# Down projection of a fused decoder step: two tiles interleaved with a lag, operands re-ordered

## What is computed

```python
def conv_ffn(h, buf, w_gate, w_up, conv_w, conv_b, w_down):
    T = h.shape[1]
    u = h @ w_gate
    upad = jnp.concatenate([buf.astype(u.dtype), u], axis=1)
    c = conv_b + sum(conv_w[j] * upad[:, j:j + T] for j in range(CONV_W))
    y = (jax.nn.gelu(c) * (h @ w_up)) @ w_down
    return y, upad[:, -(CONV_W - 1):]
```

## Time and profile before

| | |
|---|---|
| device time, median of 3 runs | 1554.88 us (1554.34 to 1556.92) |
| profiled execution, its own time | 1551.94 us |
| its span in the profile | 1550.2 us |
| instructions | 31361 |
| TensorE matmul busy | 1452.9 us (94%) |
| VectorE, ScalarE, GpSimd busy | 936.7, 675.3, 564.4 us |
| granted TensorE clock, mean | 0.977 |

### The profile page before, as it was taken

One profiled execution on the slowest core, in us unless ns is written; L12 is line 12 of the kernel. 1 busy time (PEld: TensorE's weight loads), 2 busy tenths in 40 slices (PEclk: granted clock), 3 DMA queues, 4 the chain that ended last, 5 costly groups with the idle time before them and its releaser, 6 DMA issues.

```text
span 1550.2 us, 31361 instructions
## 1 busy us (share of the span) xinstructions
PE 1452.9 (94%) x11260; PEld 1326.7 (86%) x11260; DVE 936.7 (60%) x1496; ACT 675.3 (44%) x1263; POOL 564.4 (36%) x561
## 2 busy tenths in 40 slices
PE   7999998889999999998899999998979999998997
PEld 6899898879999999997896656665969899998997
DVE  4742446579888884226647744442569988886223
ACT  5323335355666663223522444442254666664211
POOL 3332112325454443431341044441415454453343
PEclk9999999989999999999999999999989999998999
DMA  4232222213322322223221089980212322321221
GB/s 157 70 130 87 103 89 91 78 44 106 109 90 99 108 75 71 79 94 118 74 88 45 1 252 286 284 253 28 82 47 96 110 90 99 108 82 58 93 81 75
DMA packets 55608, 160.14 MB, mean 103 GB/s; under 512 B 7554, under 2 KB 25475, under 8 KB 54227
## 3 DMA queue, kind: packets, MB, share of 16 engines
q1 hardware_dynamic: 49362, 137.82, 26.8%
q0 software_dynamic: 6144, 20.98, 4.3%
HBM read 150.72 MB, written 8.05 MB: 102 GB/s over the span
## 4 chain that ended last, share of the span: by engine, by line
PE 75%; DVE 12%; issue 7%; ACT 3%; POOL 2%; ACTq 0%; POOLq 0%; DVEq 0%
PE lin L2055 33%; PE lin L2341 23%; PE lin L2519 4%; PE px L2596 2%; PE px L2560 2%; DVE a_l L1707 1%; PE px L2507 1%; PE px L2564 1%; POOL w_l L669 1%; DVE x L1516 1%; DVE tb L1510 1%; PE px L2254 1%; PE px L2527 1%; PE px L2120 1%; PE lin L2473 1%
## 5 line engine op out<-in xcount | busy, mean ns | idle before, releaser
L669 POOL TENSOR_TENSOR w_l<-w_raw,w_h 128x1024 fp32r<-128x1024 f32 (+1 forms) x62 | 172.8, 2789 | 376.4 <-ACT w_h L786 255.1
L2055 PE MATMUL lin<-xg_h,w_h 128*128 128x272 f32 x960 | 226.3, 311 | 43.0 <-DVE xg_l L1334 24.2
L2055 PE MATMUL lin<-xg_l,w_h 128*128 128x272 f32 x960 | 210.2, 294 | 0.0
L2055 PE MATMUL lin<-xg_h,w_l 128*128 128x272 f32 x960 | 210.0, 294 | 0.0
L2055 PEld LDWEIGHTS lin<-xg_h,w_h 128*128 128x128 f32 x960 | 159.5, 195 | 55.9 <-DVE xg_l L1334 17.8
L664 POOL TENSOR_TENSOR w_l<-w_raw,w_h 128x1024 fp32r<-128x1024 f32 (+2 forms) x39 | 99.4, 2549 | 222.3 <-ACT w_h L786 222.3
L2341 PE MATMUL lin<-xq_h,wq_r 128*128 128x272 f32 x864 | 176.6, 292 | 1.9 <-ACT part L1032 1.8
L786 ACT ACTIVATE w_h<-w_raw 128x1024 fp32r<-128x1024 f32 (+2 forms) x77 | 83.3, 1086 | 209.0 <-PE lin L2055 190.6
L2341 PE MATMUL lin<-xq_h,w_h 128*128 128x272 f32 x576 | 166.6, 289 | 4.1 <-DVE xq_l L1650 4.1
L2341 PE MATMUL lin<-xq_h,w_l 128*128 128x272 f32 x576 | 166.7, 289 | 0.0
L2341 PE MATMUL lin<-xq_l,w_h 128*128 128x272 f32 x576 | 166.2, 288 | 0.0
(11 more groups left out here) (360 smaller groups left out, 3125.9 us busy)
## 6 DMA issues: line engine op xcount, KB each, us to landing
wq_raw<-w SPq DMA_DIRECT2D x36, 1024.0 KB, 4.9
w_raw<-w SPq DMA_DIRECT2D x67, 512.0 KB, 3.3
w_raw<-w SPq DMA_DIRECT2D x30, 704.0 KB, 4.0
pages<-cache SPq DMA_DIRECT2D x128, 160.0 KB, 3.7
pages<-cache POOLq DMA_DIRECT2D x128, 160.0 KB, 3.7
St<-state SPq DMA_DIRECT2D x4, 1024.0 KB, 5.2
gla_s<-St SPq DMA_DIRECT2D x4, 1024.0 KB, 3.9
w_raw<-w SPq DMA_DIRECT2D x4, 576.0 KB, 4.2
```

Source lines behind the costliest of these rows:

```text
L669: g.tensor_tensor(w_l[:, p % 2, 0:n], w_raw[:, p % 2, 0:n], w_h[:, p % 2, 0:n].bitcast(F32), ALU.subtract).then_inc(w_lo, 1)
L2055: last = mm(lin[:, 2 * out_set + half, 0:HALF], w[:, slot, (w0 + k) * P:(w0 + k + 1) * P], v[:, ch, half * HALF:(half + 1) * HALF], start= ...
```

## The change

1. The high parts of operands 0, 1 and 2 get places of their own (`a_hs`: unused bytes behind `xg_l`, the place of `rstd_x`, and bytes behind `gl`; `cs` and `cb` move up by 256 bytes). They no longer wait for product 3 of the last pair.
2. ScalarE and VectorE take the 22 operands in another order in and behind the last pair, and ScalarE's `split_hi(pb+2)` comes behind all of them.
3. TensorE takes the first two down tiles together: tile 0's chunks 0 to 10, with tile 1's chunks 0 to 10 seven chunks behind (`LAG_D`), then the second halves of tile 0 and of tile 1. The order of the loads of the first four down panels follows. The hardware loop covers tiles 2 to 5; tile 6 is written out.
4. At the start of the FFN, ScalarE's `split_hi(pa+2)` comes ahead of `rstd`.
5. VectorE makes `input_lo(6)`, the last activation operand of the pairs, ahead of `sums` of pair 1 instead of behind it.

```diff
+        rstd_x_off = pos[0]
         rstd_x = keep("rstd_x", [P, 2, HALF])
...
-        cs = at("cs", E + 8736, [P, FC, NSEQ, 2])
-
+        cs = at("cs", E + 8992, [P, FC, NSEQ, 2])
+        a_hs = [at("a_h0", A0 + 32640, [P, NT], F32R), at("a_h1", rstd_x_off, [P, NT], F32R), at("a_h2", E + 6816, [P, NT], F32R)]
+        a_hs += [a_h[:, k, :] for k in range(3, FC)]
...
+        LAG_D = 7
...
-                sp_.dma_start(w_raw[:, (pb + 1) % 2, :], io["w11"][16 * layer + 1]).then_inc(raw_ready[(pb + 1) % 2], 16)
-                load_run(io["w11"], pb + 2, 16 * layer + 2, 14)
+                sp_.dma_start(w_raw[:, (pb + 1) % 2, :], io["w11"][16 * layer + 2]).then_inc(raw_ready[(pb + 1) % 2], 16)
+                load_panel(pb + 2, io["w11"][16 * layer + 1])
+                load_panel(pb + 3, io["w11"][16 * layer + 3])
+                load_run(io["w11"], pb + 4, 16 * layer + 4, 12)
...
-                    act.wait_ge(w_used, used(pb - 1) + (4 if k < 16 else 5))
+                    if k > 2:
+                        act.wait_ge(w_used, used(pb - 1) + (4 if k < 16 else 5))
...
+                split_hi(pa + 2)
                 rstd(n_stat, D, rstd_x, rstd_p)
-                split_hi(pa + 2)
...
                 part(None, j, 0)
+                operand_hi(0)
+                operand_hi(1)
                 part(None, j, 1)
                 split_hi(pb)
                 part(None, j, 2)
                 gelu(None, j - 1)
-                for k in range(2):
-                    operand_hi(k)
+                operand_hi(2)
+                operand_hi(3)
                 part(None, j, 3)
-                for k in range(2, 6):
-                    operand_hi(k)
+                operand_hi(4)
+                operand_hi(5)
                 first_tap(None, j)
                 operand_hi(6)
                 split_hi(pb + 1)
-                for k in range(7, 10):
-                    operand_hi(k)
                 gelu(None, j)
-                for k in range(10, 14):
+                for k in range(7, FC):
                     operand_hi(k)
                 split_hi(pb + 2)
-                for k in range(14, FC):
-                    operand_hi(k)
...
                 sum_lo(None, 0, 6)
+                input_lo(6)
                 sums(None, 1)
-                input_lo(6)
                 values(None, 0)
...
                 sum_lo(None, j, 6)
+                operand_lo(0)
+                operand_lo(1)
                 product(None, j - 1)
                 values(None, j)
-                for k in range(2):
-                    operand_lo(k)
+                operand_lo(2)
+                operand_lo(3)
                 up_first(None, j)
-                for k in range(2, 7):
-                    operand_lo(k)
+                operand_lo(4)
                 conv(None, j)
-                for k in range(7, 10):
-                    operand_lo(k)
+                operand_lo(5)
+                operand_lo(6)
                 product(None, j)
-                for k in range(10, FC):
+                for k in range(7, FC):
                     operand_lo(k)
...
+                for ch in range(FC // 2 + LAG_D):
+                    if ch < FC // 2:
                         pe.wait_ge(op_l, ops0 + PRODUCTS + ch + 1)
-                        last = tile_matmuls((pb + k) % 2, tb_ % 2, a_h, a_l, (ch,), w0=ch - k * FC // 2, start=ch == 0, stop=ch == FC - 1)
+                        last = tile_matmuls(pb % 2, tb_ % 2, a_hs, a_l, (ch,), w0=ch, start=ch == 0, stop=False)
+                        if ch == FC // 2 - 1:
+                            last.then_inc(w_used, 1)
+                    if ch == LAG_D:
+                        take_panel(pb + 1)
+                        free_set(tb_ + 1)
+                    if ch >= LAG_D:
+                        last = tile_matmuls((pb + 1) % 2, (tb_ + 1) % 2, a_hs, a_l, (ch - LAG_D,), w0=ch - LAG_D, start=ch == LAG_D, stop=False)
+                last.then_inc(w_used, 1)
+                for m in range(2):
+                    take_panel(pb + 2 + m)
+                    for ch in down(1):
+                        pe.wait_ge(op_l, ops0 + PRODUCTS + ch + 1)
+                        last = tile_matmuls((pb + m) % 2, (tb_ + m) % 2, a_hs, a_l, (ch,), w0=ch - FC // 2, start=False, stop=ch == FC - 1)
                     last.then_inc(w_used, 1)
...
+                with pe.Fori(0, 2) as i:
+                    for m in (2, 3):
+                        whole_tile(i, m)
+                whole_tile(None, 6)
```

More of the change, by code:

```diff
@@ L1706, in operand_lo @@
                     dve.wait_ge(op_h, ops0 + PRODUCTS + k + 1)
[L1707 removed]
+                    v.tensor_tensor(a_l[:, k, :], a[:, k, :], a_hs[k][:].bitcast(F32), ALU.subtract).then_inc(op_l, 1)
                 step.wait()
@@ L2055, in tile_matmuls @@
                             last = mm(lin[:, 2 * out_set + half, 0:HALF], w[:, slot, (w0 + k) * P:(w0 + k + 1) * P],
-                                      v[:, ch, half * HALF:(half + 1) * HALF],
+                                      (v[ch] if isinstance(v, list) else v[:, ch, :])[:, half * HALF:(half + 1) * HALF],
                                       start=start and k == 0 and m == 0, stop=stop and k == n - 1 and m == 2)
@@ L2374, in ffn @@
                 down = lambda k: range(k * FC // 2, (k + 1) * FC // 2)
-                for k in range(2):
-                    take_panel(pb + k)
-                    if k == 0:
-                        free_set(tb_)
-                        pe.wait_ge(u_out, outs0 + 2 * PAIRS - 1)
-                    for ch in down(k):
-                        pe.wait_ge(op_l, ops0 + PRODUCTS + ch + 1)
-                        last = tile_matmuls((pb + k) % 2, tb_ % 2, a_h, a_l, (ch,), w0=ch - k * FC // 2, start=ch == 0, stop=ch == FC - 1)
-                    last.then_inc(w_used, 1)
@@ L2384, in ffn @@
-                with pe.Fori(0, DC // 2 - 1) as i:
-                    for m in (1, 2):
-                        for k in range(2):
-                            pe.wait_ge(w_lo, i * 4 + lo_parts(pb + 2 * m + k + 1))
-                            if k == 0:
-                                pe.wait_ge(evac, i * 2 + (tb_ + m - 1))
-                            tile_matmuls((pb + k) % 2, (tb_ + m) % 2, a_h, a_l, down(k), start=k == 0, stop=k == 1).then_inc(w_used, 1)
+                take_panel(pb)
@@ new lines, in ffn, with whole_tile @@
+                last.then_inc(w_used, 1)
[4 more added lines that the diff above has]
+                        last = tile_matmuls((pb + m) % 2, (tb_ + m) % 2, a_hs, a_l, (ch,), w0=ch - FC // 2, start=False, stop=ch == FC - 1)
+                    last.then_inc(w_used, 1)
+                def whole_tile(i, m):
+                    for k in range(2):
+                        pe.wait_ge(w_lo, lo_parts(pb + 2 * m + k + 1) if i is None else i * 4 + lo_parts(pb + 2 * m + k + 1))
+                        if k == 0:
+                            pe.wait_ge(evac, tb_ + m - 1 if i is None else i * 2 + (tb_ + m - 1))
+                        tile_matmuls((pb + k) % 2, (tb_ + m) % 2, a_hs, a_l, down(k), start=k == 0, stop=k == 1).then_inc(w_used, 1)
@@ L2393, in ffn @@
                 free_set(tb_ + m)
-                tile_matmuls(pb % 2, (tb_ + m) % 2, a_h, a_l, down(0), start=True, stop=False).then_inc(w_used, 1)
+                tile_matmuls(pb % 2, (tb_ + m) % 2, a_hs, a_l, down(0), start=True, stop=False).then_inc(w_used, 1)
                 take_panel(pb + 2 * m + 1)
-                last_panel(pb + 2 * DC - 1, tb_ + DC - 1, n_stat + 1, a_h, a_l, down(1), False)
+                last_panel(pb + 2 * DC - 1, tb_ + DC - 1, n_stat + 1, a_hs, a_l, down(1), False)
             ffn(0, P_F0A, T_F0A, P_F0B, T_F0B, 1, 2)
```

8 lines of the change are left out of this document (5 added, 3 removed).

## The result

| | before | after |
|---|---|---|
| median | 1555.16 us (4 runs, 1554.34 to 1556.92) | **1537.16 us** (4 runs, 1537.10 to 1537.95) |
| ratio | | 0.9884, 95% interval 0.9867 to 0.9901 |
| profiled execution, its own time | 1551.94 us | 1537.11 us |
| span | 1550.2 us | 1535.4 us |
| granted TensorE clock, mean | 0.977 | 0.982 |

The median of before was 1554.88 over three runs; the fourth is 1555.44. The medians are 18.0 us apart, the two profiled executions 14.8; the one of before lies 3 us under its median. A second measurement on another chip gave 1537.23 against 1552.33, ratio 0.9898 (0.9881 to 0.9914), 15.1 us. Forecast was 14, for 1541.

What follows compares the result with a forecast made beforehand. TensorE, busy 94% of the span, was taken as the bound, losing time only to waits and lower clock. Layer 0's -6.2 and layer 1's -7.8 gave -14 off the 1554.88 median: 1541 us, range 1533 to 1549.5.

Steps and rivals of the forecast that it cites:

- Panel split ahead of rstd: Start of each FFN: TensorE's wait for w_l of panel pa+2 goes; -2.4 us in layer 0, -3.2 in layer 1.
- Last activation operand before the sums: Pairs 0 and 1: product 6's wait shrinks but pair 1's chain comes later; +1.2 us per layer, plus 0.6 for clock.
- average share of the clock: Pair 1: 0.6 us per layer added, half a slow stretch, because two waits of 2.2 lie close together.
- Places and order: Start of down projection: operands 0 to 2 ready earlier, others spread out; waits of 2.4 before chunk 5 and 0.45 remain.
- second wait of 0.45: First down tile: estimated TensorE wait while the last product's three pieces come between operands 6 and 7.
- Lag of 7: Down stage from chunk 7: two chunks per step, 1.51 us against 0.65 per operand, so the third wait (3.3) goes.
- third wait: First down tile, after chunk 13: TensorE waits until 588.05 for a_l from VectorE, counted as 3.3 us lost per layer.
- size of the down stage: Down projection: loss falls from 9.9 to 4.4 us per layer, taken as -5.6 in layer 0 and -6.4 in layer 1.
- The slow stretch: Down stage, behind its first waits: TensorE at the lower clock, charged 1.45 us in each layer.
- Rival A: Whole kernel: TensorE keeps 2.4 GHz through remaining waits and the sums' delay is hidden; -21 us, 1534; chance 0.13.
- Rival B: Panel pb+2 late, conv blocked whole, long slow stretches, one after product 4; -9 us, 1546; chance 0.22.
- Rival D: Pair loop locks into another order at GpSimd's port, period other than 10.77; slower, 1558 to 1585; chance 0.05.

Runs made afterwards that it cites:

- E1: Kernel before with only ScalarE's split of panel pa+2 moved ahead of the rstd steps; 1545.70 us, ratio to before 0.9965.
- E2: Kernel before with only VectorE's input_lo(6) moved ahead of the sums of pair 1; 1554.57 us, ratio to before 1.0021.
- E4: Changed kernel with input_lo(6) back behind the sums of pair 1; 1533.99 us beside the changed kernel's 1537.23.
- E7: E4 with w_l of panel pb+1 subtracted by VectorE instead of GpSimd, operands 7 and 8 earlier, lag 8; 1531.51 us, ratio to before 0.9864.
- E3: Changed kernel with both front edits undone (split of pa+2 and input_lo(6) as before); 1540.68 us, ratio to before 0.9926.
- E5: Changed kernel without the lag, first two down tiles one after the other; 1537.73 us beside the changed kernel's 1537.23.
- E9: Kernel before with only ScalarE's split of panel pb+2 moved behind all operands; 1543.61 us, ratio to before 0.9948.
- E6: Changed kernel with operand order and places as before, keeping the lag, its loads and both front edits; 1543.95 us, ratio to before 0.9952.
- E8: E7 with w_l of panel pb+2 also subtracted by VectorE, behind operand 17; 1528.68 us, ratio to before 0.9857.

## Why the prediction was right, and where not

The total was right (1541 forecast, 1537.2 measured, inside 1533 to 1549.5), the direction too: -14 forecast, -14.7 in the traces. By its own steps:

- *Panel split ahead of rstd*, -2.4 and -3.2: measured -2.53 and -3.29 in the traces, 5.6 alone (E1). The row was forecast for 329.05 and starts at 328.94. Right; what I had not read is that in layer 0 some 0.5 of the gain is the wait before panel pa+4.
- *Last activation operand before the sums*, +1.2 and 0.6 for a slow stretch, per layer: measured +1.19 and +2.72, and 1.15 always plus 1.56 sometimes (E2, E4). Right, chain included. A wait of 2 us that TensorE makes in pair 0 is free when pair 1 waits on a chain that VectorE's order sets. The average share of the clock was a coin toss and not a cost that each layer pays: 0 and 1.56 stand where I had 0.6 twice, and that their sum comes near is luck.
- *Places and order*: the wait of 2.4 before chunk 5 under GpSimd's `w_l` came (2.43 start to start), with the reason given (E7). The second wait of 0.45 did not come in the changed kernel; the slow stretch behind the first covered it. In layer 1 of E3 and of E4, where the clock stayed at 1.00, it came, 0.42 start to start.
- *Lag of 7*: "The third wait (3.3) goes." It went, but the sum credits the lag alone with it. The runs showed that the order removes it without the lag (E5: no loss; E9: 8.2 us by one line), and the lag without the order too (E6). In the changed kernel the lag therefore gains nothing. I had read the third wait as GpSimd's hold on the run of eight at 584.75, which is 2.5 of its 3.1 us, and had not asked why the hold fell there, nor what kept VectorE idle for 2.33 us ahead of it: that bracket names ScalarE's `a_h`, which stood behind a split waiting for TensorE. The size of the down stage, -5.6 and -6.4 against -6.06 and -6.77, was nonetheless near, since the sum only needed the wait gone.
- *The slow stretch* in the down stage, 1.45 in each layer: one stood in both, two windows at 0.50 and 0.78 in layer 0 and at 0.67 and 0.50 in layer 1. Rival A, which had it vanish, did not come true. Nor is it worth 1.45: in layer 1 of E3 and E4 it did vanish, and their last stretch, 62.94, is only 0.2 to 0.6 under the others with this order (63.10 to 63.55), because the waits that it covers come back. (Rival A's 8.1 for layer 1 is also 0.25 more than 6.4 and 1.45 make; nothing hangs on it.) The Trainium skill, TensorE: Matmul & The Clock Gate, section "HAM oscillation — how this bites in real kernels", by which it would have vanished, is contradicted by these rows again: a fall behind an idle time of 2.27 us.
- *Rival B*: panel pb+2 was not late; GpSimd ended it at 583.80 + 3.99 = 587.79, and no wait for it is in the trace. That was owed to the slow stretch, though: in layer 1 of E3 and E4 TensorE waited 0.39 for this panel. And it did not block operands 20 and 21, as forecast; VectorE's run ended at 584.71, and GpSimd stood behind it. *Rival D*: the period stayed 10.77.

The forecast's distance from the median, 4 us, is mostly that the traced execution of before was 3 us under its median and was taken off as it stood.

## What to carry to other kernels

A wait of the busiest engine that is followed by another wait on a loop-carried chain can be worth nothing, as here, and work moved ahead to remove it can cost the loop its start: follow the moved engine's queue to the next wait before pricing the first. Ask of each late operand what its *producer's* engine was queued behind; one instruction that waits in the middle of a stream of ready work cost here 8.2 us, about half of what the whole change brought. And where GpSimd and VectorE both subtract from SBUF, giving GpSimd's piece to VectorE can be cheaper for VectorE itself.

## What the runs showed that was not expected

**GpSimd mostly gets in only at the end of a run of VectorE's.** GpSimd's 128x1408 subtraction holds VectorE off for about 3.0 us (3.79 instead of 0.80 for the convolution's second half), while VectorE does the same subtraction in 1.62. In the other direction GpSimd, ready in the middle of a back-to-back run of VectorE's subtractions, mostly had to wait for the run's end: 6.42 us in E7, where none of the 13 was stretched. But not always. E1 has both outcomes in one execution, at the same place of the two layers, with GpSimd ready 2.18 us into the run of five each time:
```profile
566.79 6.26 DVE L1707 TENSOR_TENSOR a_l<-a,a_h 128x544 fp32r<-128x544 f32 x5
572.97 0.79 DVE L1577 SCALAR_TENSOR_TENSOR c<-u,par,c 128x560 f32<-128x560 f32 x1
...
568.97 3.50 POOL L664 TENSOR_TENSOR w_l<-w_raw,w_h 128x1408 fp32r<-128x1408 f32 x1 [2.39 <-ACT w_h L786]
...
1388.51 3.26 DVE L1707 TENSOR_TENSOR a_l<-a,a_h 128x544 fp32r<-128x544 f32 x5
1391.69 3.74 DVE L1577 SCALAR_TENSOR_TENSOR c<-u,par,c 128x560 f32<-128x560 f32 x1
...
1390.69 4.14 POOL L664 TENSOR_TENSOR w_l<-w_raw,w_h 128x1408 fp32r<-128x1408 f32 x1 [2.39 <-ACT w_h L786]
```
In layer 0 GpSimd enters ahead of the fifth of the five, which stands still (3.72 us by itself, from 569.33); in layer 1 it waits for the end of the run (4.14) and holds the convolution's first half (3.74). Of ten such layers in five kernels with this order, three went the first way and seven the second. This is why E6 and E9 show one wait of 3.2 where the kernel before has 1.9 and 1.2. What decides was not tried. The Trainium skill, SBUF — State Buffer, section "Who interferes with whom", says that whoever issues first holds the port pair that the two share for the whole instruction. The hold of VectorE agrees; but the 6.42 and 4.14 us of GpSimd, less the 3.2 that it needs, are longer than the rest of one instruction of 0.7.

**The length of a wait of 2 us does not decide whether the clock falls behind it.** The same wait in the middle of the program, for `xs_l`, 2.02 us long in both executions, windows of the changed kernel and then of E4:
```profile
742.00:744.00 2.00, 1.86 (x15) 1.90 (x16) 2.00 (x2) 0.00 (x0) 2.00 (x1) 1.00 0.42 168
```
```profile
742.00:744.00 2.00, 2.00 (x9) 2.00 (x10) 2.00 (x2) 0.00 (x0) 1.99 (x1) 0.50 0.20 78
```
Neither edit of E4 touches this place, and E4 is 1.5 us later behind it. Several such places in one program fit the spread of the kernel before, 1547.13 to 1555.13 on one chip, though which of them fell in which run was not counted. E8's four runs show the same: mean clock 0.987 in the two of 1526.34 and 1527.46 us, 0.980 in the two of 1529.91 and 1529.94.
